# One-core two-block Trainium2 kernel: the first block's output projection ended bank by bank, its norm run per token tile

## The reference, cut to what matters

```python
def rms_norm(x, w):
    y = xf * lax.rsqrt(jnp.mean(xf * xf, axis=-1, keepdims=True) + RMS_EPS)
    return (y * w.astype(jnp.float32)).astype(x.dtype)

# end of the first block
mixed = jnp.concatenate([moba_out, gdn_out], axis=-1) @ w_out.astype(x.dtype)
return x + rms_norm(mixed, norm_post_w)

# start of the second block
xn = rmsnorm(h, norm1_g[l])
proj = xn @ w_in[l]
```

## Time and profile before

| | us |
|---|---|
| median of 3 runs | 1301.01 |
| lowest, highest | 1300.14, 1302.89 |
| the profiled execution | 1300.44 |
| its span, first to last instruction | 1298.6 |
| mean granted TensorE clock, share of full | 0.973 |

### The profile page before, as it was taken

How to read it: one execution, slowest core, us unless ns; L and a number is a source line. 1 busy time by engine, 2 the same in 40 slices (tenths; PEclk the granted TensorE clock), 3 DMA queues, 4 the chain that set the end, 5 groups by cost and what they waited for, 6 DMA issues and landing times.

```text
span 1298.6 us, 17976 instructions
## 1 busy us (share of the span) xinstructions
PE 1232.2 (95%) x6326; PEld 1028.3 (79%) x6326; DVE 646.5 (50%) x1239; ACT 319.3 (25%) x651; POOL 650.9 (50%) x596
## 2 busy tenths in 40 slices
PE   8978999998899799999998999999999999999996
PEld 6767888887678677887787888877888888888885
DVE  3884554657571577543836565746254400244123
ACT  3125122121661304211112445431032100112001
POOL 4864342432105378665622333336566666666662
PEclk9999999999899899999987999999999999999998
DMA  6221111111001223223440111112222222222321
GB/s 241 82 81 49 49 33 49 49 33 48 33 1 65 73 82 98 81 81 100 152 130 17 52 47 53 46 49 98 83 95 97 97 97 97 97 97 97 114 81 65
DMA packets 29034, 100.39 MB, mean 77 GB/s; under 512 B 3504, under 2 KB 5936, under 8 KB 28208
## 3 DMA queue, kind: packets, MB, share of 16 engines
q1 hardware_dynamic: 26592, 91.60, 21.4%
q10 hardware_dynamic: 2384, 7.99, 2.0%
HBM read 95.39 MB, written 2.10 MB: 75 GB/s over the span
## 4 chain that ended last, share of the span: by engine, by line
PE 83%; DVE 9%; POOL 3%; issue 2%; ACT 2%; DMA 0%; DVEq 0%; SPq 0%; ACTq 0%; POOLq 0%
PE acc L267 21%; PE acc L268 20%; PE acc L269 20%; PE aux L1463 5%; PE aux L473 3%; POOL w_lo L1447 2%; PE aux L737 2%; PE aux L463 2%; PE aux L329 1%; PE acc L1566 1%; PE aux L805 1%; PE aux L806 1%; PE acc L473 1%; PE aux L768 1%; DVE conv_sum L1715 1%
## 5 line engine op out<-in xcount | busy, mean ns | idle before, releaser
L1439 POOL CAST w_hi<-w_raw 128x1024 fp32r<-128x1024 f32 x164 | 176.2, 1075 | 614.7 <-issue 445.6
L1447 POOL TENSOR_TENSOR w_lo<-w_raw,w_hi 128x256 fp32r<-128x256 f32 x352 | 286.4, 844 | 7.1
L267 PE MATMUL acc<-ht_hi,w_hi 128*128 128x512 f32 x672 | 272.5, 406 | 1.9 <-ACT token_major L899 1.1
L268 PE MATMUL acc<-ht_lo,w_hi 128*128 128x512 f32 x672 | 264.7, 394 | 0.0
L269 PE MATMUL acc<-ht_hi,w_lo 128*128 128x512 f32 x672 | 264.6, 394 | 0.0
L1442 POOL TENSOR_TENSOR w_lo<-w_raw,w_hi 128x1024 fp32r<-128x1024 f32 x76 | 188.3, 2478 | 6.1
L267 PEld LDWEIGHTS acc<-ht_hi,w_hi 128*128 128x128 f32 x672 | 128.3, 191 | 31.3 <-POOL w_lo L1447 3.7
L269 PEld LDWEIGHTS acc<-ht_hi,w_lo 128*128 128x128 f32 x672 | 127.7, 190 | 27.8
L268 PEld LDWEIGHTS acc<-ht_lo,w_hi 128*128 128x128 f32 x672 | 128.1, 191 | 25.1 <-issue 1.3
L267 PE MATMUL acc<-w_hi,ht_hi 128*128 128x512 f32 x256 | 106.0, 414 | 0.5 <-POOL w_lo L1447 0.4
L267 PE MATMUL acc<-w_hi,ff_hi 128*128 128x512 f32 x256 | 100.4, 392 | 2.3 <-POOL w_lo L1442 2.3
(11 more groups left out here) (370 smaller groups left out, 2018.4 us busy)
## 6 DMA issues: line engine op xcount, KB each, us to landing
w_raw<-units SPq DMA_DIRECT2D x164, 512.0 KB, 3.3
cmp_w<-w_kv ACTq DMA_DIRECT2D x4, 1024.0 KB, 5.8
residual<-x SPq DMA_DIRECT2D x4, 512.0 KB, 7.3
result<-normalized SPq DMA_DIRECT2D x4, 512.0 KB, 2.6
consts_sb<-consts SPq DMA_DIRECT2D x1, 1344.5 KB, 8.8
k_turned<-k_split ACTq DMA_DIRECT2D x2, 512.0 KB, 6.3
norm_post_sb<-norm_post ACTq DMA_DIRECT2D x1, 512.0 KB, 3.6
cmp_tokens<-feature_major ACTq DMA_DIRECT2D x4, 128.0 KB, 4.4
```

The costliest lines, as they stand in the source:

```text
L267: nc.tensor.matmul(bank, ah, bh, start=start, stop=False)
L268: nc.tensor.matmul(bank, ah, bl, start=False, stop=False)
L1439: nc.gpsimd.tensor_copy(w_hi[:, slot], raw[:, j]).then_inc(hi_split, 1)
L1447: done = nc.gpsimd.tensor_tensor(w_lo[:, slot, kk, cols], raw[:, j, kk, cols], w_hi[:, slot, kk, cols].bitcast(F32), ALU.subtract)
```

## The change

PE: the output projection's `Fori` is written out. Slab n = 0 stays as it was. In slab n = 1 the first two units run as before, and the last two are paired: for each bank both units' pieces, then the next bank. The waits of `opening_slab` on `post_done` become 10, 11, 12, 12. DVE: the norm's weight is scaled by -1/8192 first (the root is taken in a form without its constants), and for each tile, in order, comes `mixed` of the second half, a root of its own (eight small instructions on one column), and the three column parts of the residual; the two `flip_lo_chunk` follow the last tile. The number of matmuls is the same.

```diff
-                         lambda k: pe.wait_ge(on["post_done"], (4, 8, 12, 12)[k // 2]), 1)
+                         lambda k: pe.wait_ge(on["post_done"], (10, 11, 12, 12)[k // 2]), 1)
...
-            with pe.Fori(0, O1_SLABS) as i:
-                weight_slab(pe, i * UPS + U_O1, ht_hi, ht_lo, i + SLAB_O1, True, operand=(flip_lo, FLIP_MIXED))
+            weight_slab(pe, U_O1, ht_hi, ht_lo, SLAB_O1, True, operand=(flip_lo, FLIP_MIXED))
+            unit, slab = U_O1 + UPS, SLAB_O1 + 1
+            for j in range(2):
+                for b in range(4):
+                    weight_piece(pe, unit + j, j, b, 2 * j, ht_hi, ht_lo, slab, j == 0, False, True)
+            for b in range(4):
+                for j in (2, 3):
+                    weight_piece(pe, unit + j, j, b, 2 * j, ht_hi, ht_lo, slab, False, j == 3, True)
...
-            for n in range(O1_SLABS):
+            step(V.tensor_scalar(post_w[:], post_w[:], -1.0 / 8192, None, ALU.mult))
+
+            def mixed_out(n, b):
                 cols = slice(n * NC, (n + 1) * NC)
-                for b in range(4):
-                    eng.wait_ge(on["mixed_squares"], 4 * n + b + 1)
-                    V.tensor_tensor(mixed[:, b, cols], acc[b][:], post_w[:, cols], ALU.mult)\
-                        .then_inc(acc_out[b], 1)
-            step(V.tensor_reduce(ss, half_ss.rearrange("p (n t) -> p t n", n=2), AX, ALU.add))
-            row_norm(ss, NT, D)
-            for first, last in ((0, 256), (256, 512), (512, 1024)):
-                for t in range(NT):
-                    if first == 0:
-                        eng.wait_ge(acc_out[t], SLAB_B2)
-                    V.scalar_tensor_tensor(out=X[:, t, first:last], in0=mixed[:, t, first:last], scalar=rstd[:, t:t + 1],
+                eng.wait_ge(on["mixed_squares"], 4 * n + b + 1)
+                V.tensor_tensor(mixed[:, b, cols], acc[b][:], post_w[:, cols], ALU.mult).then_inc(acc_out[b], 1)
+
+            def root_of_mixed(t):
+                v, h, y = ss[:, t:t + 1], tmp4[:, t:t + 1], post_y[t]
+                step(V.tensor_scalar(v, half_ss[:, t:t + 1], half_ss[:, 4 + t:5 + t], 1.0 / D, ALU.add, ALU.mult))
+                step(V.tensor_scalar(y.bitcast(I32), v.bitcast(I32), -0.5, float(0x5f3759df),
+                                     ALU.mult, ALU.add))
+                for three in (3.0, 12.0, 768.0):
+                    step(V.scalar_tensor_tensor(out=h, in0=v, scalar=y, in1=y, op0=ALU.mult, op1=ALU.mult))
+                    step(V.scalar_tensor_tensor(out=y, in0=h, scalar=-three, in1=y, op0=ALU.add, op1=ALU.mult))
+
+            for b in range(4):
+                mixed_out(0, b)
+            step(V.tensor_scalar(half_ss[:, 0:4], half_ss[:, 0:4], D * EPS, None, ALU.add))
+            for t in range(NT):
+                mixed_out(1, t)
+                root_of_mixed(t)
+                eng.wait_ge(acc_out[t], SLAB_B2)
+                for first, last in ((0, 256), (256, 512), (512, 1024)):
+                    V.scalar_tensor_tensor(out=X[:, t, first:last], in0=mixed[:, t, first:last], scalar=post_y[t],
                                            in1=X[:, t, first:last], op0=ALU.mult,
                                            op1=ALU.add).then_inc(on["post_done"], 1)
-                if first == 256:
-                    for k in range(2):
-                        flip_lo_chunk(eng, ht_hi, ht_lo, k, FLIP2, lambda k: param("norm1", k))
+            for k in range(2):
+                flip_lo_chunk(eng, ht_hi, ht_lo, k, FLIP2, lambda k: param("norm1", k))
```

More of the change, by code:

```diff
@@ L419, in two_blocks @@
         half_ss = small(340, 8)
+        post_y = [small(356 + t, 1) for t in range(NT)]
         go_ss, go_rs, t32, nega = small(272, 16), small(288, 16), small(304, 32), small(336, 4)
```

## The result

| | before | changed |
|---|---|---|
| median of 6 runs, us | 1300.98 | 1307.43 |
| lowest, highest | 1300.14, 1302.89 | 1304.98, 1309.85 |
| profiled execution, us | 1300.44 | 1307.45 |
| span | 1298.6 | 1305.6 |

The changed kernel takes 1.0046 times the time before (95% interval 1.0032 to 1.0061): slower by 6.5 us, or 7.0 in the profiled executions. PE's waits from 380 us on in the changed kernel (total, times, longest) answer to the earlier trace rows: the wait in front of the transposes has grown from 7.2 to 9.9 us, and a new one on `w_lo` of 2.7 us stands beside it.

What follows compares the result with a forecast made beforehand. PE, busy for 95% of the span, was taken as the bound, losing time in its wait before the second block's first transposes. 1300.44 + 7.85 - 0.1 = 1308.2 profiled, 1308.8 by the median; range 1303.6 to 1312.0.

Steps and rivals of the forecast that it cites:

- F: Start of the second block's first transposes on PE; forecast at 448.95, 7.85 us later than 441.10.
- The stall (1): Output projection, slab 1, bank 0: PE must wait for POOL's split of the fourth unit, a stall of 2.95 us.
- The clock (2): PE's matmuls behind the stall run at a lower clock, 1.73 us more; bounds nothing or 1.73 us.
- The queue (3): DVE needs 3.90 us a tile against PE's 2.72 a bank, so it falls behind by 1.2 us a tile.
- The turns (4): POOL's splits of the second block's units alternate with DVE's root and residual, mainly tile 2: 4.1 us added.
- sharing of bandwidth: DVE beside POOL: alternative that the engines do not exclude each other for whole instructions; time near 1304.
- Behind F (5): After the second block's first transposes: nothing later, clock back 5.8 us behind them, chunk 4's transposes saving 0.1 us.
- W: Start of PE's first matmul behind the second block's first transposes; forecast 3.53 us behind them, at 452.5.
- A: Rival at DVE's tiles: a queue without turn-taking, POOL's splits hardly meeting DVE; 1304.7 or 1303.9 us; chance 0.13.
- B: Rival at DVE's tiles: POOL in the way of tile 3 as well; 1311.7 us; chance 0.07.
- C: Rival at bank 0: no stall, fourth unit ready in time, first transposes at today's 441.06; 1301.0 us; chance 0.04.
- D: Rival at the projection's end: faster, DVE's tail shrinks to one tile; 3.6 us less, 1297.4; chance 0.03.

Runs made afterwards that it cites:

- e1: Kernel before with only PE's half of the change, the last two units paired bank by bank: median 1307.91 us, ratio 1.0047.
- e3: Changed kernel, POOL's split of the next slab's first unit held until tile 3's first residual part is done: median 1307.26 us, ratio 1.0048.
- e4: Changed kernel with PE's last eight pieces reordered so the fourth unit is wanted later, without the stall: median 1307.55 us, ratio 1.0047.
- e9: Changed kernel with 11 and 30 unread matmuls keeping the clock up, and POOL's split held until tile 3's first residual part: 1303.35 us, ratio 1.0018.
- e8: Changed kernel with unread matmuls keeping the clock up, 11 in PE's stall and 40 before the first transposes: median 1305.93 us, ratio 1.0033.
- e5: Kernel before, POOL's split of the next slab's second unit held until the residual is complete: median 1298.58 us, ratio 0.9979.
- e6: Kernel before with 28 unread matmuls in the gap before the first transposes, keeping the clock up: median 1300.73 us, ratio 0.9997.
- e10: Kernel before with second unit's split held, 20 unread matmuls in the gap, and the residual's last 512 columns in two parts: 1301.01 us, ratio 0.9999.
- e2: Changed kernel with PE's old loop, so only DVE's half, root and residual per tile: median 1305.31 us, ratio 1.0031.

## Why the prediction was right

It forecast 1308.8 us in a range of 1303.6 to 1312.0; measured 1307.43. The mechanism is the one forecast. The number is closer than its parts: F came 0.8 us later than forecast, and 1.9 us came back behind it, of which 0.1 was forecast. That the two partly cancel is luck. Point by point:

*The stall (1).* PE went on 3.94 us behind POOL's cast; 427.18 - 423.19 = 3.99 were forecast. Confirmed.

*The clock (2).* Right in kind, wrong in size. Against the kernel's end where it fell 0.7 us after PE went on, the clock here fell 0.6 us before PE could go on, and stayed low until 433.6. The 42 matmuls took 439.94 - 427.36 = 12.58 us, 3.06 over full pace, where 1.73 were taken from the kernel's end. This is the mis-sized term, and it made bank 3 late by 1.3 us. It is a matter of the execution, for behind the same stall the 42 matmuls were 1.74 us over full pace in e1 (11.26) and 1.45 in e3 (438.67 - 427.70 = 10.97). At F the low clock weighed 1.65 us in the changed kernel and 1.22 in e3, where the forecast had estimated 0.8 from bank 0's end.

*The queue (3).* 3.84 us a tile against 3.90. e4 shows that it does not need the stall: with PE unhindered, F is still 7.15 us later. Only the wait of tile 1 for ACT (0.36 us) was new, from the longer low clock.

*The turns (4).* Tile 2 took 7.82 us against 8.05 forecast, tile 3 2.91 against 2.86. The splits fell on nearly the instructions named: four were lengthened before the second cast where three were forecast, with 0.65 us for those beside `w_lo`, and the one beside that cast took 0.94. That it is POOL, three pairs show: e3 takes 3.99 us off tile 2, e9 against e8 4.65 off tiles 1 and 2, and e5 brings F 1.74 us forward in the kernel before. The prediction set against sharing of bandwidth the rule of the Trainium skill's page SBUF — State Buffer (section Who interferes with whom), by which one engine is shut out for the other's whole instruction. The trace agrees: with bandwidth only shared F would be near 444.8, and it was at 449.96. The introduction says that the engines meet only at semaphores; DVE and POOL meet here where no semaphore stands between them.

*Behind F (5).* W moved exactly as F. The step that was off is the clock's return, which I kept at 5.8 us behind F. It came at 454.0, 4.1 us behind. By their starts F is 8.86 us later (0.23 were there at the cast), and chunk 4 7.93 (455.21 against 447.28), so 0.93 came back. The clock alone could not have given that: before, chunk 4 started when DVE's last residual part had ended (444.50 + 2.73 = 447.23), and e6 shows PE waiting 0.99 us for it at full clock. In the changed kernel that part is done at 450.96, ahead of PE. The forecast had seen this wait as 0.1 us, because it left the clock as it was. Two further spells of low clock, 200 and 400 us on, moved as well. The 64 small matmuls of L737 (L738 in the changed kernel) took 13.91 us before, all at low clock, and 11.70 after, where the clock fell only 2.5 us behind their start. In the kernel before:

```profile
645.06 13.91 PE L737 MATMUL aux<-cmp_blocks,cmp_w 128*128 128x62 f32 x64 [2.65 <-DVE cmp_blocks L1189]
...
706.18 0.35 PE L805 MATMUL aux<-k_split,q_split_even 128*128 128x128 f32 x1 [3.13 <-DVE q_split_even L1286]
...
863.62 1.97 PE L329 MATMUL aux<-consts_sb,y_b 128*128 128x128 f32 x16 [0.45 <-DVE y_b L538]
```

and in the changed one:

```profile
652.97 11.70 PE L738 MATMUL aux<-cmp_blocks,cmp_w 128*128 128x62 f32 x64 [2.66 <-DVE cmp_blocks L1190]
...
712.15 0.30 PE L806 MATMUL aux<-k_split,q_split_even 128*128 128x128 f32 x1 [3.13 <-DVE q_split_even L1287]
...
870.03 3.30 PE L329 MATMUL aux<-consts_sb,y_b 128*128 128x128 f32 x16 [0.45 <-DVE y_b L539]
```

The delay of 7.91 us at the first row has shrunk to 5.97 at the second. At the third the 16 transposes run at low clock in the changed kernel alone, and at the kernel's last stall the delay is 6.98 (1285.98 against 1279.00). So 8.86 us at F became 7.0 in the profiled execution.

*The rivals.* A would have needed the 4 us of tile 2 away, which is e3; B's tile 3 was not held; C's stall came, and e4, which has no stall, puts F 7.15 us later and not at today's place: its bank 0 ends 3.2 us later than in C's sum, and POOL costs 4.2 us on tiles 0 and 1, which C left out; D's condition, DVE under 2.72 us a tile, was missed by 1.1 us.

What stays open: why equal programs differ in their low-clock spells from run to run, by up to 5 us in e3. The runs that are longer have the lower mean clock; which stretch they lose it in was not looked at in more than one execution of each kernel. Whether the 1.9 us that came back behind F belong to the change or to that one execution is open too.

## What to carry to other kernels

Before work is cut into pieces so that a second engine can start earlier, compare the second engine's time for a piece with the first one's: here 3.84 us against 2.72, so it became a queue, and one shared root had been cheaper than four. Ask of every reordering which buffer now comes free at another moment, and what the engine behind that buffer will then do beside the tail: POOL's splits were worth more (4.0 us at F) than the low clock behind PE's stall (1.7), and in e10's timeline they are back in another place as soon as PE is a microsecond earlier. A transfer or a split that is not due yet can be held back with one wait; that alone made this kernel 0.2% faster than it was.

## What the runs showed of the hardware that was not expected

- The root's first two instructions, one tensor and constants or column scalars on 128x1 values, are not lengthened beside POOL. In e2 they take 0.20 and 0.15 us (435.83, 436.06) while `w_lo` runs from 434.84 to 437.93; on 128x4 values the same kind took 0.65 beside it. Two-input ones beside `w_lo` are lengthened in both shapes, most of them to 0.65.
- A stall of 2.31 us was followed by about 3.4 us of low clock at the kernel's end. A stall of 2.74 us was followed by 6.8 us of it in the changed kernel (426.7 to 433.6), which began before PE went on, and by 3.4 us in e1 and in e3.
- The low clock behind a gap of 7.35 us costs this kernel 0.6 us at the first matmul behind it and not 2, because the next engine's chain is nearly as long as PE's slow work (e6).
